# Paged sample attention: one block of scores per sequence, laid over four groups of 32 rows, in place of four blocks of 32 rows

## Chip, cores and metric

The kernel is one inference step of a decoder layer on one core of a Trainium2 chip. The metric is device time in microseconds (us), the median of several executions. Engines are named as in the profile: PE (TensorE matmul), PEld (its weight load), DVE (VectorE), ACT (ScalarE), POOL (GpSimd), SP (the engine that issues most DMAs).

## What is computed

The layer has a front projection, attention for a prompt of 1024 rows, attention for 8 sample sequences against paged caches, an output projection and an expert layer. The change is in the sample attention alone. In the reference it is, for each of the 8 sequences (16 pages of 128 cached rows, 4 new positions, 8 heads):

```python
def one_seq(args):
    pages, qb, cb, rb = args
    c_past = cache_kv_latent[pages].reshape(-1, KV_LORA)
    r_past = cache_k_rope[pages].reshape(-1, QK_ROPE_DIM)
    ...
    k = mla_keys(c_all, r_all, w_uk, g_k_nope, g_k_rope)
    mask = jnp.arange(past + s)[None, :] <= (past + jnp.arange(s))[:, None]
    p = attn_probs(qb[None], k, mask)
    o_lat = jnp.einsum('bhql,blc->bqhc', p.astype(c_all.dtype), c_all)
    return jnp.einsum('bqhc,chv->bqhv', o_lat, w_uv)[0]
```

`mla_keys` normalises each key over 96 numbers, of which 64 come from the latent row through `w_uk` and 32 from the rotary cache. `attn_probs` is a softmax over 2052 columns. All data is float32.

## The kernel before

`sample_attention` handles the 8 sequences b one after the other, each in 16 page steps p. The 4 positions by 8 heads make SQ = 32 query rows. PE makes, for each page, the page's keys of all heads (`d_kn`, line 786: two matmuls with 512 columns, into one of two PSUM banks) only to get their norms: ACT squares them (`d_sq`, line 883, two buffers) and DVE sums them per head (line 948). The scores themselves are made without the keys, from queries that were multiplied with `w_uk` ahead (`d_qa`): every fourth page, `group(c)` makes the scores of four pages in three matmuls of 512 columns into 32 rows of one of two banks (lines 777 and 778), and ACT copies them to `s_row` (line 889), 32 rows of 2052 columns.

The softmax of a sequence is its tail, and runs a piece at a time within the page steps of the next sequence: each engine's `tail` returns a table from page number to piece. On PE: the inverse norms are turned page by page into rows (line 812, 16 matmuls at pages 1 and 2), the probabilities are turned page by page (line 827, 16 matmuls at page 6), the latent rows are multiplied with them (lines 837 and 838, 17 matmuls of 256 columns at page 7), the result is turned (line 844, page 9). On DVE: four products of scores and norms (line 972), the row maximum (986), 1/sum and the scaling of the result (993, 997). ACT takes the exponential (line 904).

Within DVE's page steps stand the steps of the expert gather, 20 per sequence: each waits for a 512 KB row block that POOL fetched with an indirect DMA (line 126) into one of five buffers, and takes one pass over it (lines 141 and 148); POOL fetches into a buffer once DVE has used it.

SP issues the page loads. `load_keys` (line 728) issues 32 DMAs for a sequence, `load_latents` (lines 732 and 734) 17. The keys of sequence n+1 are issued once the scores of sequence n-1 are made, since both use one of two buffers; its latents once the latent product of n-1 is made (`d_lat`). PE begins the stage when `d_w_ukT` has landed (semaphore `d_ukt`), and waits at page 4 of the first sequence for the other 12 pages of keys. Order on each engine is the order written here; nothing reorders it.

Of the kernel before, what the change touches and what calls it, by code (L numbers as in the profile page):

```python
# [16 lines left out]
P = 128  # L17
# [633 lines left out]
def sample_attention(nc, a, qk_s, kept, gather, steps, gelus):  # L651
# [3 lines left out]
    SQ = DEC_S * H  # L655
    with ExitStack() as ctx:
        def sb(name, shape, dt=F32):
# [4 lines left out]
        w_ukT = sb("d_w_ukT", [NOPE, H, KVL])  # L662
        eps = sb("d_eps", [P, 1])
# [12 lines left out]
        s_new = [sb(f"d_snew{e}", [DEC_S, SQ]) for e in range(2)]  # L676
        rows = [sb(f"d_rows{e}", [P, PAST + DEC_S]) for e in range(2)]
        s_row = [r[0:SQ, :] for r in rows]
        mx = sb("d_mx", [SQ, 1])
        nmx = sb("d_nmx", [SQ, 1])  # L680
        tot = sb("d_tot", [SQ, 1])
        inv = sb("d_inv", [SQ, 1])
        pT = sb("d_pT", [P, PAGES + 1, SQ])
        ol = sb("d_ol", [SQ, KVL])
        olT = sb("d_olT", [P, CT, H, NS])
        o = rows[0][0:NS, 0:H * VD]
        oT = rows[0][:, 512:512 + G4 * P].rearrange("p (k t) -> p k t", k=G4)
# [6 lines left out]
        s = with_sems(nc, ctx, """d_first0 d_first1 d_rest0 d_rest1 d_lt0 d_lt1 d_eps d_qg d_qap d_qa d_mm d_sq d_red d_sc d_raw d_krsq d_krss  # L694
            d_ks1 d_ks2 d_ks3 d_kinv d_new d_smask d_tr d_nb d_ntr d_nrow d_mx d_nmx d_exp d_inv d_ptr d_pt d_lat d_ol
            d_olt d_olT d_op d_o d_ot d_zero d_oT d_st d_ukt""")
# [3 lines left out]
        GROUPS = PAGES // 4  # L700
# [18 lines left out]
        def _(sp):  # L719
# [29 lines left out]
            sp.dma_start(a["mixT_d"][:, :, SEQ:NPAD], oT).then_inc(s["d_st"], 16)  # L749
# [7 lines left out]
        def _(pe):  # L757
            pe.wait_ge(s["d_qg"], 2)
            pe.wait_ge(s["d_ukt"], 16)
# [7 lines left out]
            def pages(b, e, n, tail):  # L767
                cols = slice(b * DEC_S, (b + 1) * DEC_S)
                some = slice(b * SQ, (b + 1) * SQ)

                def group(c):

                    after(pe, s["d_raw"], GROUPS * b + c - 1)
                    o = sc[c % 2][0:SQ, :].rearrange("q (p l) -> q p l", l=P)
                    four = slice(4 * c, 4 * c + 4)
                    for k in range(CT):
                        pe.matmul(o, qa[:, k, some], page[e][:, four, k * P:(k + 1) * P], start=k == 0, stop=False)
                    pe.matmul(o, qr[:, some], krT[e][:, four, :], start=False, stop=True).then_inc(s["d_sc"], 1)
                for p in range(PAGES):
# [9 lines left out]
                    if p % 4 == 3:  # L789
                        group(p // 4)  # L790
# [1323 lines left out]
```

## Time and profile before

| | |
|---|---|
| median of 3 executions | 3730.46 us (3698.07 to 3737.71) |
| profiled execution: span from first to last instruction | 3729.2 us |
| PE busy | 3092.1 us (83%) |
| DVE busy | 2760.2 us (74%) |
| POOL, ACT busy | 1769.9 us, 992.3 us |
| DMA over the span | 241 GB/s, 899.72 MB |
| sample attention | from about 952 to 1481 us of the span |

The profile gives of the profiled execution only its span; what lies around it is not shown, and the span stands 1.3 us below the median of the three. Times in the rows below are from the start of the span. In a row of instructions the first number is the start, the second the time covered, then engine, line, operation, output and inputs, shapes, and how many records were merged. A float32 matmul leaves two MATMUL records and two weight loads. An idle time ahead of a row stands in brackets with what ended it. A share of busy time is an average, so the stage's own rows are what counts here.

### The profile page before, as it was taken

Reading aid. Unit: us, or ns where it says so; the run is one execution under the profiler, and the core shown is the slowest. Engines: PE = TensorE matmul, PEld = TensorE weight load, DVE = VectorE, ACT = ScalarE, POOL = GpSimd, SP = SyncE. Lnnn points to the kernel's source line nnn. Section 1 sums busy time; section 2 is a strip of 40 time slices with the busy share of each in tenths; the row PEclk is TensorE's granted clock in tenths of the full one; section 3 lists DMA queues with packets and bytes.
Section 4 is the critical chain, followed back from the end, with each engine's and each line's share of the span. In section 5 each row is a group of like instructions: output and inputs, shape, how many; then the busy total and the mean of one; then the engine's idle time right before and its main releaser. Section 6 shows DMA issues by size and latency. Waiting matters only on the chain. (4 is left out here: it accounts for less than half of the span.)

```text
span 3729.2 us, 41634 instructions
## 1 busy us (share of the span) xinstructions
PE 3092.1 (83%) x13229; PEld 2245.2 (60%) x13229; DVE 2760.2 (74%) x5323; ACT 992.3 (27%) x1643; POOL 1769.9 (47%) x1379
## 2 busy tenths in 40 slices
PE   6655687887699997765774779999999999999997
PEld 3445344565344443434764667777777877787775
DVE  3237687578567673673999877888888888898887
ACT  2222122233223232111111663222222222222221
POOL 0025554256333341563564554556666655555553
PEclk9577798578799998777887899999999999999998
DMA  3221576378787773886100359999999999999987
GB/s 111 88 102 45 202 274 218 116 228 291 251 282 254 241 251 117 307 314 218 34 23 6 137 242 333 343 328 333 339 341 330 343 330 336 336 341 340 331 330 262
DMA packets 311725, 899.72 MB, mean 241 GB/s; under 512 B 34377, under 2 KB 125690, under 8 KB 301242
## 3 DMA queue, kind: packets, MB, share of 16 engines
q0 software_dynamic: 156672, 570.49, 43.3%
q1 hardware_dynamic: 152874, 323.74, 24.2%
q10 hardware_dynamic: 2016, 3.67, 0.3%
q8 instruction: 59, 0.97, 0.1%
q14 instruction: 104, 0.85, 0.1%
HBM read 844.38 MB, written 53.64 MB: 241 GB/s over the span
## 5 line engine op out<-in xcount | busy, mean ns | idle before, releaser
L126 POOL DMA_INDIRECT x_got<-v,x_expert x544 | 676.8, 1244 | 750.1 <-DVE x_y L148 609.4
L126 POOL DMA_INDIRECT x_got<-u_rows,x_expert x544 | 731.8, 1345 | 626.2 <-DVE x_got L141 477.7
L148 DVE SCALAR_TENSOR_TENSOR x_y<-x_got,x_hidden,x_y 128x1024 f32<-128x1024 f32 x544 | 695.4, 1301 | 40.7 <-DMA x_got<-v,x_expert 31.7
L141 DVE SCALAR_TENSOR_TENSOR x_got<-x_got,x_y 128x1024 f32<-128x1024 f32 x544 | 646.8, 1220 | 37.9 <-DMA x_got<-u_rows,x_expert 36.5
L1735 PE MATMUL e_a<-h2h,e_uh 128*128 128x512 f32 x1024 | 406.5, 397 | 53.9 <-DVE e_ul L1815 34.3
L1737 PE MATMUL e_a<-h2h,e_ul 128*128 128x512 f32 x1024 | 401.1, 392 | 0.0
L1736 PE MATMUL e_a<-h2l,e_uh 128*128 128x512 f32 x1024 | 400.7, 391 | 0.0
L1780 ACT ACTIVATE e_vh<-e_v 128x2048 fp32r<-128x2048 f32 x64 | 122.5, 1915 | 567.6 <-PE e_yt L1754 544.7
L1735 PEld LDWEIGHTS e_a<-h2h,e_uh 128*128 128x128 f32 x1024 | 193.4, 189 | 115.3 <-issue 57.6
L786 PE MATMUL d_kn<-w_uk_kept,d_page 128*128 128x512 f32 x512 | 254.6, 641 | 9.5 <-DMA d_krT<-page_krT 8.7
L1737 PEld LDWEIGHTS e_a<-h2h,e_ul 128*128 128x128 f32 x1024 | 193.3, 189 | 41.1
L1736 PEld LDWEIGHTS e_a<-h2l,e_uh 128*128 128x128 f32 x1024 | 193.5, 189 | 38.7
L1752 PE MATMUL e_y<-e_wh,e_vh 128*128 128x512 f32 x512 | 201.6, 394 | 5.8 <-DVE e_wl L1835 5.7
L1754 PE MATMUL e_y<-e_wh,e_vl 128*128 128x512 f32 x512 | 200.5, 392 | 0.0
L1753 PE MATMUL e_y<-e_wl,e_vh 128*128 128x512 f32 x512 | 200.4, 391 | 0.0
L1753 PE MATMUL e_yt<-e_wl,e_vh 128*128 128x512 f32 x512 | 199.6, 390 | 0.0
L1752 PE MATMUL e_yt<-e_wh,e_vh 128*128 128x512 f32 x512 | 199.6, 390 | 0.0
L948 DVE TENSOR_REDUCE d_kss<-d_sq 128x8 f32<-128x512 f32 x128 | 87.0, 679 | 152.0 <-ACT d_sq L883 152.0
L1754 PE MATMUL e_yt<-e_wh,e_vl 128*128 128x512 f32 x512 | 199.3, 389 | 0.0
L1821 DVE TENSOR_TENSOR e_vl<-e_v,e_vh 128x2048 fp32r<-128x2048 f32 x64 | 146.4, 2288 | 44.4 <-ACT e_vh L1780 44.4
L1815 DVE TENSOR_TENSOR e_ul<-e_u,e_uh 128x1024 fp32r<-128x1024 f32 x128 | 156.6, 1223 | 28.5 <-ACT e_uh L1775 28.2
L786 PEld LDWEIGHTS d_kn<-w_uk_kept,d_page 128*128 128x128 f32 x512 | 96.7, 200 | 131.8 <-issue 119.8
(394 smaller groups left out, 5937.8 us busy)
## 6 DMA issues: line engine op xcount, KB each, us to landing
e_u<-uT SPq DMA_DIRECT2D x128, 512.0 KB, 6.9
e_v<-v SPq DMA_DIRECT2D x64, 1024.0 KB
gates_d<-g_stage SPq DMA_DIRECT2D x8, 4096.0 KB, 11.8
e_gate<-gates_d SPq DMA_DIRECT2D x32, 1024.0 KB
d_page<-page SPq DMA_DIRECT2D x128, 144.0 KB, 3.5
d_latent<-page_rows SPq DMA_DIRECT2D x128, 128.0 KB
x_got<-u_rows,x_expert POOLq DMA_INDIRECT x544, 5.9
x_got<-v,x_expert POOLq DMA_INDIRECT x544, 6.0
```

The source lines that it names most:

```text
L126: pool.indirect_dma_start(out=self.got[row][:], out_offset=None, in_=self.tables[phase], in_offset=bass.IndirectOffsetOnAxis(ap=self.exper ...
L141: dve.scalar_tensor_tensor(out=row[:], in0=row[:], scalar=1.0, in1=self.y[g][:], op0=ALU.mult, op1=ALU.mult, accum_out=self.hidden[:, g, k ...
L148: dve.scalar_tensor_tensor(out=self.y[g][:], in0=row[:], scalar=self.hidden[:, g, k:k + 1], in1=self.y[g][:], op0=ALU.mult, op1=ALU.add).t ...
L786: mm = pe.matmul(kn[p % 2][:, :], page[e][:, p, k * P:(k + 1) * P], w_uk[:, k, :], start=k == 0, stop=k == CT - 1)
L1735: pe.matmul(o, uh[q][:, k, :], h2h[:, k, :], start=k == 0, stop=False)
L1736: pe.matmul(o, uh[q][:, k, :], h2l[:, k, :], start=False, stop=False)
L1737: mm = pe.matmul(o, ul[q][:, k, :], h2h[:, k, :], start=False, stop=k == KD - 1)
L1752: pe.matmul(o, h, wh[r][:, :], start=begins and c == 0, stop=False)
L1753: pe.matmul(o, h, wl[r][:, :], start=False, stop=False)
L1754: mm = pe.matmul(o, l, wh[r][:, :], start=False, stop=ends and c == 3)
L1815: dve.tensor_tensor(ul[r][:], u[j % U_RING][:], uh[r][:].bitcast(F32), ALU.subtract).then_inc(s["e_ul"], 1)
L1821: dve.tensor_tensor(vl[:, two, :], v[:], vh[:, two, :].bitcast(F32), ALU.subtract).then_inc(s["e_vl"], 1)
```

## The change

The 128 partitions are cut into PARTS = 4 groups of 32 rows, and page 4c+j belongs to group j, block c. The scores of a sequence are no longer made in four blocks: after its last page PE makes them all in 12 matmuls of 512 columns, which write group j of one bank, so that `s_row` has 128 rows of 516 columns. The inverse norms and the probabilities are then turned by four whole 128x128 transposes each. The latent product has the same 17 matmuls, but block c of group j adds into rows 32j to 32j+31 of `lat`. Since a query's scores now stand in four rows, its maximum and its sum have to be joined over groups. For the maximum PE turns the 128 row maxima into one row (`maxima`), DVE takes the maximum over the groups (`top`), PE spreads it (`spread`, four matmuls) and ACT scales it (`nmx`). For the sum there is one matmul with a constant matrix `same`, which is loaded by a new DMA that PE waits for at the start of the stage. The matmuls that turn the result join the groups through `same` too. ACT copies the scores once per sequence, and the tail's pieces stand at other pages.

```diff
+    PARTS = P // SQ
+    GROUPS = PAGES // PARTS
...
+        same = sb("d_same", [P, P])
...
-        s_row = [r[0:SQ, :] for r in rows]
+        s_row = sb("d_rows", [P, GROUPS * P + DEC_S])
+        prob = sb("d_prob", [P, GROUPS * P + DEC_S])
+        top = sb("d_top", [1, SQ])
+        pT = sb("d_pT", [P, GROUPS, P])
...
-        sc = [bank("d_sc0"), bank("d_sc1")]
-        misc = [bank("d_m0"), bank("d_m1")]
+        sc = bank("d_sc")
+        norm = bank("d_nb")
+        turn = bank("d_pt")
         new = bank("d_new")
         lat = bank("d_lat")
+        small = bank("d_small")
+        new_sc = new[0:DEC_S, 0:SQ]
+        new_turn = new[:, P:P + DEC_S]
+        new_prob = new[0:DEC_S, 2 * P:2 * P + SQ]
+        mx_row, mx_col, tot_col = small[0:1, 0:P], small[:, P:P + 1], small[:, 2 * P:2 * P + 1]
...
             load_keys(0, 0)
+            sp.dma_start(same[:], a["same"]).then_inc(s["d_ukt"], 16)
             load_keys(1, 1)
             load_latents(0, 0)
             load_latents(1, 1)
             for n in range(1, DEC_B - 1):
                 e = (n - 1) % 2
                 sp.wait_ge(s["d_krsq"], n)
-                sp.wait_ge(s["d_raw"], GROUPS * n)
+                sp.wait_ge(s["d_sc"], n)
...
+                after(pe, s["d_raw"], b)
+                for k in range(CT):
+                    for j in range(PARTS):
+                        pe.matmul(sc[j * SQ:(j + 1) * SQ, :].rearrange("q (c l) -> q c l", l=P), qa[:, k, some],
+                                  page[e][:, j:PAGES:PARTS, k * P:(k + 1) * P], start=k == 0, stop=False)
+                for j in range(PARTS):
+                    mm = pe.matmul(sc[j * SQ:(j + 1) * SQ, :].rearrange("q (c l) -> q c l", l=P), qr[:, some],
+                                   krT[e][:, j:PAGES:PARTS, :], start=False, stop=True)
+                mm.then_inc(s["d_sc"], 1)
             def tail(t, e, n):
...
+                def new_rows():
+                    pe.wait_ge(s["d_smask"], t + 1)
+                    pe.wait_ge(s["d_neg"], 2)
+                    after(pe, s["d_nrow"], t)
+                    pe.matmul(new_turn, s_new[e][:], ident[0:DEC_S, 0:DEC_S], start=True,
+                              stop=True).then_inc(s["d_ntr"], 1)
+                def norms():
                     pe.wait_ge(s["d_kinv"], t + 1)
...
+                    after(pe, s["d_nb"], t)
+                    for c in range(GROUPS):
+                        mm = pe.transpose(norm[:, c * P:(c + 1) * P],
+                                          kinv[:, c * PARTS:(c + 1) * PARTS, :].rearrange("p j q -> p (j q)"), ident[:])
                     mm.then_inc(s["d_tr"], 1)
...
+                def maxima():
+                    pe.wait_ge(s["d_mx"], t + 1)
+                    after(pe, s["d_inv"], t)
+                    pe.matmul(mx_row, mx[:], ident[:], start=True, stop=True).then_inc(s["d_mxr"], 1)
+                def spread():
+                    pe.wait_ge(s["d_top"], t + 1)
+                    after(pe, s["d_nmx"], t)
+                    for j in range(PARTS):
+                        mm = pe.matmul(mx_col[j * SQ:(j + 1) * SQ, :], top[:], ident[0:1, 0:1], start=True, stop=True)
+                    mm.then_inc(s["d_mxc"], 1)
                 def probs():
                     pe.wait_ge(s["d_exp"], t + 1)
...
+                    after(pe, s["d_pt"], t)
+                    for c in range(GROUPS):
+                        mm = pe.transpose(turn[:, c * P:(c + 1) * P], prob[:, c * P:(c + 1) * P], ident[:])
                     mm.then_inc(s["d_ptr"], 1)
...
+                    after(pe, s["d_ptn"], t)
+                    pe.matmul(new_prob, prob[0:SQ, GROUPS * P:GROUPS * P + DEC_S], ident[0:SQ, 0:SQ], start=True,
+                              stop=True).then_inc(s["d_ptr"], 1)
+                    after(pe, s["d_inv"], t)
+                    pe.matmul(tot_col, same[:], tot[:], start=True, stop=True).then_inc(s["d_totc"], 1)
                 def latent():
                     pe.wait_ge(latent_in[e], 16 * (PAGES + 1) * n)
...
+                    pe.wait_ge(s["d_pt"], t + 1)
+                    pe.wait_ge(s["d_ptn"], t + 1)
+                    after(pe, s["d_olT"], t)
+                    pe.matmul(lat[0:SQ, 0:KVL], pT_new[:], c_now[e][:], start=True, stop=False)
+                    for c in range(GROUPS):
+                        for j in range(PARTS):
+                            mm = pe.matmul(lat[j * SQ:(j + 1) * SQ, 0:KVL], pT[:, c, j * SQ:(j + 1) * SQ],
+                                           latent_rows[e][:, c * PARTS + j, :], start=c == 0 and j > 0,
+                                           stop=c == GROUPS - 1)
+                    mm.then_inc(s["d_lat"], 1)
                 def latent_turn():
                     pe.wait_ge(s["d_ol"], t + 1)
                     for k in range(CT):
...
+                        mm = pe.matmul(lat[:, KVL + k * SQ:KVL + (k + 1) * SQ], ol[:, k * P:(k + 1) * P],
+                                       same[:, 0:SQ], start=True, stop=True)
                     mm.then_inc(s["d_olt"], 1)
-                return {1: norms_first, 2: norms_rest, 6: probs, 7: latent, 9: latent_turn}
+                return {2: new_rows, 3: norms, 5: maxima, 6: spread, 9: probs, 11: latent, 13: latent_turn}
...
+                def raw():
+                    act.wait_ge(s["d_sc"], t + 1)
+                    after(act, s["d_exp"], t)
+                    act.activation(s_row[:, 0:GROUPS * P], sc[:, :], ACT.Copy).then_inc(s["d_raw"], 1)
...
+                    act.wait_ge(s["d_mxc"], t + 1)
+                    act.activation(nmx[:], mx_col, ACT.Copy, scale=-SM).then_inc(s["d_nmx"], 1)
+                    act.wait_ge(s["d_nmx"], t + 1)
                     act.wait_ge(s["d_nrow"], t + 1)
...
+                    after(act, s["d_ptr"], 2 * t)
+                    after(act, s["d_totc"], t)
+                    act.activation(prob[:], s_row[:], ACT.Exp, bias=nmx[:], scale=SM,
...
-                return {3: row_new, 5: exp, 7: probs, 10: latent_turn}
+                return {1: raw, 3: row_new, 7: exp, 10: probs, 14: latent_turn}
...
+                    dve.tensor_tensor(s_row[:, 0:GROUPS * P], s_row[:, 0:GROUPS * P], norm[:, :],
                                       ALU.mult).then_inc(s["d_nb"], 1)
...
+                    dve.wait_ge(s["d_nb"], t + 1)
+                    dve.wait_ge(s["d_nrow"], t + 1)
+                    after(dve, s["d_mxr"], t)
+                    dve.tensor_reduce(mx[:], s_row[:], AX, ALU.max).then_inc(s["d_mx"], 1)
                 def maximum():
...
+                    dve.wait_ge(s["d_mxr"], t + 1)
+                    after(dve, s["d_mxc"], t)
+                    dve.tensor_reduce(top[:], mx_row.rearrange("o (j q) -> o q j", j=PARTS), AX,
+                                      ALU.max).then_inc(s["d_top"], 1)
                 def latent():
...
+                    dve.wait_ge(s["d_totc"], t + 1)
+                    dve.reciprocal(inv[:], tot_col).then_inc(s["d_inv"], 1)
                     dve.wait_ge(s["d_inv"], t + 1)
                     dve.wait_ge(s["d_lat"], t + 1)
                     after(dve, s["d_olt"], t)
...
-                return {2: scaled_first, 3: scaled_rest, 4: maximum, 9: latent}
+                    dve.tensor_scalar(ol[:], lat[:, 0:KVL], inv[:], None, ALU.mult).then_inc(s["d_ol"], 1)
+                return {4: scaled, 6: maximum, 12: latent}
...
+        "same": np.tile(np.eye(DEC_S * H, dtype=f), (P // (DEC_S * H), P // (DEC_S * H))),
```

How the order moves, at the three places that matter. First PE, pages 1 to 7 of the second sequence, before (`d_m` holds turned norms and probabilities, `d_sc` scores, `d_lat` the latent product):

```order
L786 MATMUL d_kn<-w_uk_kept,d_page 128x512 x2
L812 MATMUL d_m<-ident_kept,d_kinv 32x128 x8
L786 MATMUL d_kn<-w_uk_kept,d_page 128x512 x2
L812 MATMUL d_m<-ident_kept,d_kinv 32x128 x8
L821 MATMUL d_new<-ident_kept,d_snew 32x4
L786 MATMUL d_kn<-w_uk_kept,d_page 128x512 x2
L777 MATMUL d_sc<-d_page,d_qa 32x512 x2
L778 MATMUL d_sc<-d_krT,d_qr 32x512
L786 MATMUL d_kn<-w_uk_kept,d_page 128x512 x6
L827 MATMUL d_m<-ident_kept,d_rows 128x32 x16
L830 MATMUL d_m<-ident_kept,d_rows 4x32
L786 MATMUL d_kn<-w_uk_kept,d_page 128x512 x2
```

The tail is done by page 9 there, and two of the four blocks of scores stand between its pieces.

The same sequence on PE after the change, from page 3 to page 11 (`d_nb` turned norms, `d_pt` turned probabilities, `d_small` maxima and sums):

```order
L825 MATMUL d_nb<-ident_kept,d_kinv 128x128 x4
L788 MATMUL d_kn<-w_uk_kept,d_page 128x512 x4
L832 MATMUL d_small<-ident_kept,d_mx 1x128
L788 MATMUL d_kn<-w_uk_kept,d_page 128x512 x2
L838 MATMUL d_small<-ident_kept,d_top 32x1 x4
L788 MATMUL d_kn<-w_uk_kept,d_page 128x512 x6
L845 MATMUL d_pt<-ident_kept,d_prob 128x128 x4
L848 MATMUL d_new<-ident_kept,d_prob 4x32
L851 MATMUL d_small<-d_tot,d_same 128x1
L788 MATMUL d_kn<-w_uk_kept,d_page 128x512 x4
L858 MATMUL d_lat<-d_c_now,d_pTn 32x256
L861 MATMUL d_lat<-d_latent,d_pT 32x256 x16
```

Sixteen matmuls for the norms and sixteen for the probabilities became four transposes each, the latent product moved from page 7 to page 11, and the pieces at pages 5 and 6 are new. Behind it, from page 12 to the end of the sequence:

```order
L788 MATMUL d_kn<-w_uk_kept,d_page 128x512 x4
L869 MATMUL d_lat<-d_same,d_ol 128x32 x2
L788 MATMUL d_kn<-w_uk_kept,d_page 128x512 x4
L805 MATMUL d_sc<-d_page,d_qa 32x512 x8
L808 MATMUL d_sc<-d_krT,d_qr 32x512 x4
```

The 12 score matmuls stand in one lump behind the last page.

DVE, the tail of the first sequence inside the second, after the change, with the gather steps (`x_got`) between:

```order
L976 TENSOR_REDUCE d_kss<-d_sq 128x8
L1000 TENSOR_TENSOR d_rows<-d_rows,d_nb 128x512
L1005 TENSOR_REDUCE d_mx<-d_rows 128x1
L141 SCALAR_TENSOR_TENSOR x_got,x_hidden<-x_got,x_y 128x1024
L976 TENSOR_REDUCE d_kss<-d_sq 128x8
L141 SCALAR_TENSOR_TENSOR x_got,x_hidden<-x_got,x_y 128x1024
L976 TENSOR_REDUCE d_kss<-d_sq 128x8
L1010 TENSOR_REDUCE d_top<-d_small 1x32
```

The four products at pages 2 and 3 became one at page 4 with the maximum right behind it, and the joined maximum `d_top` stands two pages later.

SP, after the change, at the end of the first sequence's keys:

```order
L738 DMA d_page<-page 128x288
L738 ISA
L738 DMA d_krT<-page_krT 32x128
L748 DMA d_same<-same 128x128
L732 TENSOR_LOAD table_kept
```

The load of `same` stands behind all 32 key loads of the first sequence; the one of `d_w_ukT` stands ahead of them as before.

## Rows read from the trace of the kernel before

**Rows 1.** Busy time in stretches of the stage; the first line names the columns
```profile
core 0: us, PE busy (x) PEld busy (x) DVE busy (x) ACT busy (x) POOL busy (x), PEclk, DMA share, GB/s
1018.50:1079.70 61.20, 60.28 (x214) 26.04 (x212) 41.97 (x72) 19.46 (x32) 24.11 (x21) 0.97 0.85 286
...
1140.70:1201.70 61.00, 60.08 (x209) 26.63 (x208) 41.86 (x50) 18.26 (x31) 23.32 (x21) 0.94 0.76 250
...
1445.70:1480.00 34.30, 24.44 (x136) 17.78 (x136) 7.25 (x11) 4.68 (x8) 0.00 (x0) 0.75 0.07 26
```

**Rows 2.** Waits, 960 to 1460 us: who waited for whom, total, times, longest
```profile
ACT d_sq L883 <- PE d_kn L786: 227.4, 107, 11.9
POOL x_got L126 <- DVE x_y L148: 218.5, 91, 12.7
DVE d_kss L948 <- ACT d_sq L883: 152.0, 41, 14.8
```

**Rows 3.** Timeline of PE, pieces of the second sequence
```profile
1018.95 1.99 PE L786 MATMUL d_kn<-w_uk_kept,d_page 128*128 128x512 f32 x4
1020.86 0.54 PE L795 MATMUL d_new<-qk_s 96*4 96x4 f32 x16
...
1023.25 1.93 PE L812 MATMUL d_m<-ident_kept,d_kinv 128*32 128x128 f32 x16
...
1030.92 1.90 PE L777 MATMUL d_sc<-d_page,d_qa 128*32 128x512 f32 x4
...
1033.72 5.42 PE L786 MATMUL d_kn<-w_uk_kept,d_page 128*128 128x512 f32 x12
1039.81 3.75 PE L827 MATMUL d_m<-ident_kept,d_rows 32*128 32x32 f32 x32 [0.67 <-ACT d_rows L904]
...
1043.52 3.66 PE L786 MATMUL d_kn<-w_uk_kept,d_page 128*128 128x512 f32 x4
...
1049.91 7.09 PE L837 MATMUL d_lat<-d_latent,d_pT 128*32 128x256 f32 x32
```

**Rows 4.** Transposes of 128x128 in the prompt attention, timeline of PE
```profile
887.01 1.04 PE L577 MATMUL t2a_t<-t2a_ident,t2a_p 128*128 128x128 f32 x8
```

**Rows 5.** Groups by line, 960 to 1460 us: busy us, mean ns, idle before
```profile
L148 DVE SCALAR_TENSOR_TENSOR x_y<-x_got,x_hidden,x_y 128x1024 f32<-128x1024 f32 x122 | 155.6, 1275 | 2.6
L948 DVE TENSOR_REDUCE d_kss<-d_sq 128x8 f32<-128x512 f32 x128 | 87.0, 679 | 152.0 <-ACT d_sq L883 152.0
L972 DVE TENSOR_TENSOR d_rows<-d_rows,d_m 32x512 f32<-32x512 f32 x32 | 20.4, 668 | 3.4 <-PE d_m L812 3.4
L986 DVE TENSOR_REDUCE d_mx<-d_rows 32x1 f32<-32x2052 f32 x8 | 18.2, 2269 | 0.0
```

**Rows 6.** Timeline of SP: first and last key load of a sequence, its latents
```profile
1091.27 0.33 SPq L728 DMA_DIRECT2D d_page<-page  x1
...
1116.73 0.33 SPq L728 DMA_DIRECT2D d_krT<-page_krT  x1
...
1120.43 17.09 SPq L734 DMA_DIRECT2D d_latent<-page_rows  x16
```

**Rows 7.** DMA queues, 960 to 1460 us: packets, MB, share of 16 engines
```profile
q0 software_dynamic: 22896, 83.37, 49.8%
q1 hardware_dynamic: 42546, 37.35, 23.9%
```

**Rows 8.** Timeline at the start of the stage, PE and SP
```profile
957.52 7.00 PE L762 MATMUL d_kn<-d_qg,d_w_ukT 64*128 64x32 f32 x32 [10.81 <-DMA d_w_ukT<-w_ukT]
...
980.53 0.33 SPq L728 DMA_DIRECT2D d_krT<-page_krT  x1
...
986.28 4.63 PE L786 MATMUL d_kn<-w_uk_kept,d_page 128*128 128x512 f32 x5 [8.73 <-DMA d_krT<-page_krT]
```

**Rows 9.** Timeline at its end: last score matmul on PE, last turned result on ACT
```profile
1441.93 1.04 PE L778 MATMUL d_sc<-d_krT,d_qr 32*32 32x512 f32 x2
...
1477.46 0.22 ACT L917 ACTIVATE d_olT<-d_m 128x64 f32<-128x64 f32 x1 [10.77 <-PE d_m L844]
```

More of the change, by code:

```diff
@@ L769, in pages @@
                 some = slice(b * SQ, (b + 1) * SQ)
[L771 to L778, printed above, removed]
                 for p in range(PAGES):
@@ L794, in pages @@
                         for h in range(H):
[L795 removed]
+                            mm = pe.matmul(new_sc[:, h * DEC_S:(h + 1) * DEC_S], qk_s[0:HD, H + h, cols],
                                            qk_s[0:HD, h, cols], start=True, stop=True)
@@ L799, in pages @@
                         tail[p]()
-            def tail(t, e, n):
-                def norms_first():
-                    pe.wait_ge(s["d_kinv"], t + 1)
-                    after(pe, s["d_olT"], t)
-                    after(pe, s["d_pt"], 2 * t)
-                    norms(0)
-                    norms(1)
-                def norms(c):
-                    for p in range(4 * c, 4 * c + 4):
-                        mm = pe.matmul(misc[c % 2][0:SQ, (p % 4) * P:(p % 4 + 1) * P], kinv[:, p, :], ident[:],
-                                       start=True, stop=True)
-                    mm.then_inc(s["d_tr"], 1)
-                def norms_rest():
-                    for c in (2, 3):
-                        pe.wait_ge(s["d_nb"], GROUPS * t + c - 1)
-                        norms(c)
-                    pe.wait_ge(s["d_smask"], t + 1)
-                    pe.transpose(new[0:SQ, 2 * SQ:2 * SQ + DEC_S], s_new[e][:],
-                                 ident[0:DEC_S, 0:DEC_S]).then_inc(s["d_ntr"], 1)
+                after(pe, s["d_raw"], b)
@@ L824, in probs @@
                 def probs():
                     pe.wait_ge(s["d_exp"], t + 1)
-                    for p in range(PAGES):
-                        mm = pe.matmul(misc[0][:, p * SQ:(p + 1) * SQ], s_row[e][:, p * P:(p + 1) * P],
-                                       ident[0:SQ, 0:SQ], start=True, stop=True)
+                    after(pe, s["d_pt"], t)
+                    for c in range(GROUPS):
+                        mm = pe.transpose(turn[:, c * P:(c + 1) * P], prob[:, c * P:(c + 1) * P], ident[:])
@@ L833, in latent @@
                 def latent():
                     pe.wait_ge(latent_in[e], 16 * (PAGES + 1) * n)
-                    pe.wait_ge(s["d_pt"], 2 * t + 2)
-                    for p in range(PAGES):
-                        pe.matmul(lat[0:SQ, 0:KVL], pT[:, p, :], latent_rows[e][:, p, :], start=p == 0, stop=False)
-                    pe.matmul(lat[0:SQ, 0:KVL], pT[0:DEC_S, PAGES, :], c_now[e][:], start=False,
-                              stop=True).then_inc(s["d_lat"], 1)
+                    pe.wait_ge(s["d_pt"], t + 1)
@@ L935, in _ @@
                               ALU.mult).then_inc(s["d_qg"], 1)
+            for e in range(2):
+                dve.memset(s_new[e][:], NEG).then_inc(s["d_neg"], 1)
+            dve.memset(oT[:], 0.0).then_inc(s["d_zero"], 1)
             def pages(b, e, n, tail):
```

94 lines of the change are left out of this document (28 added, 66 removed).

## The prediction

> **What bounds the kernel now.** I read the busy times by stretch first. In a sequence of the sample attention PE is busy 60 of 61 us, DVE 42, POOL 23, and the DMA engines 0.76 to 0.85 of the time [rows 1]. The waits say the same: ACT waited 227 us for PE's page keys, DVE 152 us for ACT's squares, and POOL 218 us for DVE to give back a buffer [rows 2], while DVE's pass over a fetched block had 2.6 us of idle time ahead of it in all [rows 5]. So PE paces this stage, the gather follows, and work taken from PE is worth time there until DVE, SP's issuing or the DMA engines take over. The stages behind it only start earlier. Seven sequences run from 1018.95 us [rows 3] to the end of the last scores at 1442.97 us [rows 9], which is 60.6 us for each.
>
> **PE per sequence.** A page is four records, 12 of them take 5.42 us [rows 3], so 1.77 us for a page with its handover and 28.3 us for 16. The scores cost per block 1.9 for four records and 0.93 for two more [rows 3, 9], 11.2 us in all. Norms cost 2 x 1.9, probabilities 0.67 + 3.75, the page behind them 3.66 in place of 1.77, since the granted clock was at the lower level there, the latent product 7.6 with the new row, and the rest about 1.3 [rows 3]. The sum is 58.
>
> After the change the page keys stay at 28.3. Norms and probabilities become four transposes each, and four took 1.04 us [rows 4]. The small pieces (maxima, spread, the sum through `same`, the new row) are under 20 records; 16 tiny records took 0.54 us [rows 3], so 0.7 us, and with `d_new` and the turned result 1.8 us. The scores still are 24 records of 512 columns and the latent product 34 of 256. What four column groups do is not in this trace: no two matmuls here write different groups of 32 rows. Above, they run one after the other: 24 x 0.46 = 11 us and 7.6 us, as now [rows 3]. Below, four at a time: 2.8 and 2 us. I take a value between. A float32 matmul is two records over the same columns, so the second of one matmul cannot share its columns' group with the first, but can run beside the first record of the next group's matmul. 24 records then fill 13 slots, 6 us, and 34 fill 18, 4 us. PE's sum is 28.3 + 2.1 + 1.8 + 6 + 4 = 42 us (51 with no overlap, 37 with full overlap).
>
> The Trainium skill (TensorE: Matmul & The Clock Gate, part 3, on packing small matmuls) says that matmuls in different column groups run at once but start and end in program order, and gives 2.38x for three column tiles. By that factor, as an estimate, the scores would take 4.7 us; no run here shows it, and the sequence's time below would be the same.
>
> **DVE per sequence.** It was busy 41.9 us [rows 1]. Four products of 0.668 us over 32 rows become one of the same width over 128 rows, and the maximum of 2052 columns, 2.27 us, becomes one of 516, about the 0.68 us of a 512-column reduction [rows 5]. With a small one for `top` (0.2) that is 4.9 - 1.6 = 3.3 us less: 38.6. Two places add about 1.5 us: the maximum must wait for the product just ahead of it, and the Sqrt on ACT at the sequence's end is waited for as now. That makes 40.
>
> **The new waits.** At page 5 PE waits for DVE's maximum, which stands behind DVE's page 3, and at page 6 for `top`, behind DVE's pages 4 and 5. Behind it on PE are pages 6 and 7, which DVE will want. DVE then holds two pages of squares not yet summed and up to three gather steps, 1.28 + 0.68 us a page [rows 5], so some 4 us of work, while PE needs 1.8 us for a page and ACT another 0.6: covered as long as fetched blocks are there. Without that cover it would cost some 2 us a sequence. The ACT chain behind it (scale, Exp) has three pages until PE's probabilities at page 9. The scores' lump holds back the next page 0 by 6 us; DVE has its last two pages, the end of the sequence and a gather step, about 8 us, to do in the meantime. With 11 us of lump it would stand idle some 5 us.
>
> **SP.** A sequence's 32 key loads take 1091.27 to 1117.06, 25.8 us, and its 17 latent loads 18.4 us [rows 6], together 44 us per sequence at the least. The latents now start behind page 11 and not 7: at about 33 us of a 48 us sequence, ending at 52, so the next keys start 4 us late. They are wanted 48 us after that sequence's start and need 26, so this hides.
>
> **DMA.** Over 500 us the two queues took 49.8% and 23.9% of the 16 engines [rows 7], that is 368 us, or 46 us per sequence. None of this traffic goes away. So 46 us is the floor if the engines never pause, above DVE's 40, SP's 44 and PE's 42. The highest share in these stretches is 0.85 [rows 1], which would make 54 us, but PE was holding the gather back there. I take 48 (0.96 busy), nearer to the floor, since five buffers of fetches and SP's loads compete at all times. With the two bounds the range for a sequence is 46 to 54.
>
> **Start and end.** PE now waits for `same` too. It is issued behind the keys whose last load goes out at 980.53 us, and those keys had landed at 986.28 [rows 8], so PE starts at about 987 and not 957.5. It then does its 7 us of queries, ACT copies them, and page 0 runs at the lower clock (a page took 3.66 at it [rows 3]): DVE gets its first squares at about 999.5. All keys are there by then, so 16 pages at DVE's pace of 36 us (no tail inside yet) and the lump end at about 1037. Before, it was 1018.95: a loss of 18 us, bounded by 15 and 23 (no overlap). At the end, the last tail has no pages to hide in. It took 1442.97 to 1477.68, 34.7 us [rows 9]. The change takes from it 2.8 us for norms, 2 for products, 1.6 for the maximum, 2.7 for probabilities, 3.6 for latents [rows 3 to 5] and 1.4 for an exponential a quarter as wide, and adds about 2 us of handovers for the joined maximum: 12 us less (8 with no overlap).
>
> **Sum.** +18 - 7 x (60.6 - 48) - 12 = -82 us. The span of 3729.2 becomes 3647; the median shown lies 1.3 us above the span, so 3648.
>
> **Rivals.**
> 1. The column groups do not overlap, and the change buys only what the transposes and the wider tail give. For it: nothing in the trace shows two groups at once. PE has 51 us of work and some 2 us of waits for DVE: 53 us a sequence. +22 - 7 x 7.6 - 8 = -39: 3691.
> 2. PE's clock. The page behind the probabilities ran at 1.2 GHz, 3.66 us in place of 1.77 [rows 3], and in the stage's end, with PE busy 24.4 of 34.3 us, the granted clock was 0.75 against 0.94 to 0.97 [rows 1]. PE now waits at pages 5 and 6 and idles more, so more pages may run at the lower level. Each costs 1.9 us. With no overlap and 53 us a sequence, the kernel gets slower from 58.6 us on, at three such pages; six make 64.4 us, +22 + 7 x 3.8 - 8 = +41: 3771. With overlap it takes over nine pages to lose anything. Against it: where PE has work it stays near 0.95, and with no overlap it has work nearly all the time.
> 3. The DMA engines stay at 0.85, as fetches through five buffers leave gaps: 54 us, +18 - 46 - 12 = -40: 3690. Against it: in no stretch was the gather itself waited for [rows 2, 5].
>
> **How the numbers follow.** The forecast, with overlap at least in pairs and 46 to 51 us a sequence (3632 to 3669), has 0.60; rival 1 has 0.25 (3680 to 3705), rival 2 has 0.08, rival 3 has 0.07. Start and end unknowns widen the forecast to 3620 on the low side. The range of 3620 to 3704 leaves out rival 2 and the edges of the others. About 1% is what can be told from no change, so faster means below 3693: all of the forecast, half of rival 1 and most of rival 3, 0.76; within 1%, 0.16; slower, rival 2, 0.08.
>
> **What would show it.** Right: sequences start 48 us apart, DVE's waits for ACT's squares nearly vanish, the DMA share is 0.9 or more in every sequence, the 24 score records take about 6 us and the 34 latent records 4, and PE's first matmul of the stage starts near 987. Wrong: the 24 records take 10 us or more (rival 1), pages of 3.6 us in number (rival 2), DVE waiting for fetched blocks at a DMA share of 0.85 (rival 3).

## The result, and the profile after

The changed kernel takes 3601.8 us (median of 4 executions, 3584.1 to 3612.8) where the kernel before took 3717.9 (median of 4; three of them gave the 3730.5 from which the forecast was worked out). The ratio is 0.967, with a 95% interval of 0.963 to 0.971: faster, as forecast, and by more than the range allowed (low end 3620). Medians and ratios below are of executions in the faster of two states; one of experiment 6, 9649 us, is left out by that.

In the profiled executions below the sample attention starts anywhere from 917.8 to 956.9 us of the span with the same work ahead of it, so whole times of single executions scatter. What is compared below is therefore the **stage**: from SP's issue of `d_w_ukT` to ACT's last `d_olT`. Before, it ran from 952.74 to 1477.46 us [rows 9], 524.7 us; after, from 956.9 to 1355.38, 398.5 us. The span fell by 118.2 us (3729.2 to 3611.0), 8 less than the stage: the stage begins 4.2 us later, and some 4 are lost behind it. A **gap** is the time from one sequence's rotary score matmuls to the next's; it was 60.6 us before.

Of the stage's -126.2 us, the first sequence brought +7.2 (its lump ends 73.4 us behind the stage's start, before 66.2), the seven gaps -115.5 (41.2, 41.6, 41.6, 47.0, 45.2, 47.0, 44.8: mean 44.1) and the last tail -17.9 (16.8 us for 34.7). The prediction had +18, -88 and -12.

The busy times by stretch of the kernel after, columns as in [rows 1]; the first stretch is the second sequence, the last one lies in the sixth and seventh:

```profile
1030.26:1071.51 41.25, 37.26 (x170) 15.84 (x166) 39.09 (x70) 15.59 (x29) 25.68 (x21) 1.00 1.05 385
1071.51:1113.10 41.59, 37.27 (x171) 15.85 (x167) 39.74 (x48) 15.04 (x28) 24.70 (x21) 1.00 1.02 360
1200.00:1250.00 50.00, 44.22 (x204) 18.40 (x197) 41.63 (x52) 17.27 (x32) 27.41 (x22) 0.93 0.96 340
```

Against [rows 1], PE is down from 60 to 37 us a sequence and DVE from 42 to 39. The number to look at is the next to last: the DMA share passes 1.0 at 385 GB/s, where before 0.85 stood beside 286 GB/s. Later the granted clock falls a little (0.93) and the rate too, as PE pauses there.

PE in that second sequence, columns as in [rows 3]:

```profile
1040.16 0.60 PE L825 MATMUL d_nb<-ident_kept,d_kinv 128*128 128x128 f32 x4
...
1045.13 0.38 PE L832 MATMUL d_small<-ident_kept,d_mx 128*1 128x128 f32 x2 [0.94 <-DVE d_mx L1005]
...
1048.80 0.24 PE L838 MATMUL d_small<-ident_kept,d_top 1*32 1x1 f32 x8 [1.37 <-DVE d_top L1010]
...
1054.22 0.60 PE L845 MATMUL d_pt<-ident_kept,d_prob 128*128 128x128 f32 x4
...
1055.14 3.68 PE L788 MATMUL d_kn<-w_uk_kept,d_page 128*128 128x512 f32 x8
1058.75 0.61 PE L858 MATMUL d_lat<-d_c_now,d_pTn 4*32 4x256 f32 x2
1059.29 1.93 PE L861 MATMUL d_lat<-d_latent,d_pT 128*32 128x256 f32 x32
1061.16 3.70 PE L788 MATMUL d_kn<-w_uk_kept,d_page 128*128 128x512 f32 x8
...
1068.67 1.92 PE L805 MATMUL d_sc<-d_page,d_qa 128*32 128x512 f32 x16
1070.52 1.06 PE L808 MATMUL d_sc<-d_krT,d_qr 32*32 32x512 f32 x8
1071.51 1.98 PE L788 MATMUL d_kn<-w_uk_kept,d_page 128*128 128x512 f32 x4
```

The 24 score records take 2.84 us from the start of the first to the start of the next page: the time of six, so four groups at once. The 32 latent records take 1.87 us to the next row's start (2.41 with the new row), where they took 7.09 before [rows 3]. The page behind the probabilities no longer runs at half the clock: there 8 records take 3.68 us, where 4 took 3.66 [rows 3]. The two waits for the joined maximum (0.94 and 1.37 us) are there, as foretold, and DVE did not wait for PE's pages behind them.

From the fourth sequence on, PE waits at page 4 in every one:

```profile
1124.42 5.40 PE L788 MATMUL d_kn<-w_uk_kept,d_page 128*128 128x512 f32 x8 [2.57 <-DMA d_krT<-page_krT]
```

The waits of the kernel after, 956 to 1356 us (who waited for whom, total, times, longest) [rows 2]:

```profile
ACT d_sq L908 <- PE d_kn L788: 191.7, 106, 10.5
POOL x_got L126 <- DVE x_y L148: 105.9, 74, 6.4
DVE d_kss L976 <- ACT d_sq L908: 63.2, 17, 38.9
PE d_kn L773 <- DMA d_same<-same: 36.4, 1, 36.4
PE d_kn L788 <- DMA d_krT<-page_krT: 26.7, 5, 6.8
```

DVE's wait for squares fell from 152 to 63 us, 38.9 of it one wait at the start. New is the last line: five waits for keys, one in each of sequences 4 to 8. Who makes the keys late stands in SP's timeline, first and last key load of a sequence, its latents and the next first key load [rows 6]:

```profile
1094.46 0.33 SPq L738 DMA_DIRECT2D d_page<-page  x1
...
1119.68 0.33 SPq L738 DMA_DIRECT2D d_krT<-page_krT  x1
...
1121.41 17.08 SPq L744 DMA_DIRECT2D d_latent<-page_rows  x16
1139.32 0.33 SPq L738 DMA_DIRECT2D d_page<-page  x1
```

SP waited for nothing inside the stage. A sequence's 49 issues take it from 1094.46 to 1139.32, 44.9 us, and the later loads up to 46.0; the last four gaps have a mean of 46.0. The last keys go out at 1119.68 and PE has them at 1124.42, where its wait ends, 4.7 us later; in the next four sequences it is 5.6 or 5.7 us. Nor is it traffic that slows the issuing: the first 32 key loads of the stage went out in 25.6 us (958.72 to 984.32) at 132 GB/s, these 32 in 25.6 (1094.46 to 1120.05) at 377.

The DMA queues, 960 to 1340 us, columns as in [rows 7]:

```profile
q0 software_dynamic: 22741, 82.82, 59.9%
q1 hardware_dynamic: 43232, 37.88, 31.7%
```

The same 121 MB moved, in 380 us and not 500, at a share that rose only from 74 to 92%. PE's timeline at the start of the stage and at its last scores [rows 8, 9]:

```profile
986.41 7.00 PE L773 MATMUL d_kn<-d_qg,d_w_ukT 64*128 64x32 f32 x32 [36.42 <-DMA d_same<-same]
...
1337.80 1.06 PE L808 MATMUL d_sc<-d_krT,d_qr 32*32 32x512 f32 x8
```

PE now starts 29.5 us behind the stage's begin, having waited for `same`. ACT's last turned result, which closes the stage [rows 9]:

```profile
1355.38 0.22 ACT L942 ACTIVATE d_olT<-d_lat 128x64 f32<-128x64 f32 x1 [5.96 <-PE d_lat L869]
```

From the start of the last scores to it are 17.6 us; before, there were 35.5 [rows 9].

### The profile page after: what moved, and what is told of

It is laid out like the page before. It is cut to its first block and busy times, and to the rows that moved or that the text cites. A ratio compares the mean times of both kernels' runs of the same rounds, so it can differ in the third digit from the quotient of the medians.

```text
span 3611.0 us, 40929 instructions
## 1 busy us (share of the span) xinstructions
PE 2940.8 (81%) x12893; PEld 2175.4 (60%) x12893; DVE 2731.0 (76%) x5301; ACT 966.1 (27%) x1627; POOL 1772.3 (49%) x1379
## 5 line engine op out<-in xcount | busy, mean ns | idle before, releaser
L126 POOL DMA_INDIRECT x_got<-v,x_expert x544 | 684.1, 1258 | 627.7 <-DVE x_y L148 480.8
L148 DVE SCALAR_TENSOR_TENSOR x_y<-x_got,x_hidden,x_y 128x1024 f32<-128x1024 f32 x544 | 695.6, 1302 | 45.2 <-DMA x_got<-v,x_expert 35.8
L788 PE MATMUL d_kn<-w_uk_kept,d_page 128*128 128x512 f32 x512 | 251.4, 635 | 29.7 <-DMA d_krT<-page_krT 26.7
L1866 DVE TENSOR_TENSOR y_turned<-e_yt,y_turned 128x512 f32<-128x512 f32 x124 | 85.6, 690 | 100.5 <-PE e_yt L1774 100.5
```

The lines of the kernel that those rows point to most:

```text
L126: pool.indirect_dma_start(out=self.got[row][:], out_offset=None, in_=self.tables[phase], in_offset=bass.IndirectOffsetOnAxis(ap=self.exper ...
L148: dve.scalar_tensor_tensor(out=self.y[g][:], in0=row[:], scalar=self.hidden[:, g, k:k + 1], in1=self.y[g][:], op0=ALU.mult, op1=ALU.add).t ...
L788: mm = pe.matmul(kn[p % 2][:, :], page[e][:, p, k * P:(k + 1) * P], w_uk[:, k, :], start=k == 0, stop=k == CT - 1)
```

## Experiments

The theory after the result was **A**: SP's issuing paces the sequences from the fourth on, and the first three escape it because their loads went out while PE waited 36 us for `same`. Its rivals were **B** (the start's 36 us add to the end) and **C** (the DMA engines' bandwidth is the bound, at a share near 1).

**1. `same` issued ahead of the first keys** (B against A)

```diff
-            load_keys(0, 0)
             sp.dma_start(same[:], a["same"]).then_inc(s["d_ukt"], 16)
+            load_keys(0, 0)
             load_keys(1, 1)
```

> The load of `same` is issued right behind `d_w_ukT`, ahead of the keys, so PE can start near 961 us in place of 986. Theory A (SP's issuing paces the stage: 44.7 us of issuing per sequence without a pause from 957 us on): the keys of sequences 3 to 8 arrive when they did, so the stage ends where it did and the time equals the changed kernel's within 4 us; PE waits longer for keys (26.7 us in 5 waits becomes about 40). Theory B (the start's delay is simply added to the end): 11 to 15 us less than the changed kernel. Theory C (the DMA engines are the bound): also no change, but without longer waits for keys.

Measured: 3597.8 us, 0.968 [0.962, 0.974]; the stage 398.5 us, as long as the change's. PE began 24.5 us earlier against the stage's start, and its waits for keys grew instead, from 26.7 us in 5 to 50.0 in 8 (gaps 42.6, 51.2, then 44.0 to 47.5). B falls: the start was no cost, the loads' own pace set the end.

**2. Less issuing on SP** (A against C): a third latent buffer, so that the latents of a page go out with its keys, and one reading of the page's number serves three DMAs. The bytes are the same.

```diff
-        latent_rows = [sb(f"d_latent{e}", [P, PAGES, KVL]) for e in range(2)]
+        latent_rows = [sb(f"d_latent{e}", [P, PAGES, KVL]) for e in range(3)]
...
-                load_keys(n + 1, e)
-                sp.wait_ge(s["d_lat"], n)
-                load_latents(n + 1, e)
+                after(sp, s["d_lat"], n - 1)
+                load(n + 1, True, True)
```

> A third buffer of latent rows, so that SP issues a sequence's latents together with its keys and reads each page number once for three DMAs: about 36 us of issuing per sequence in place of 44.7, same bytes. Theory A (SP paces): the waits for keys vanish and all sequences take the 41.3 us that the first two took, DVE being the next bound: 7 x 2.7, about 18 us less than the changed kernel (12 to 22). Theory C (DMA engines, whose busy share is 0.96 to 1.05 now, are the bound): no change, within 4 us.

Measured: 3572.6 us, 0.959 [0.953, 0.965]; the stage 379.5, 19.0 shorter, and the gaps 40.2 to 42.9 us. SP's timeline, from the first issue of one sequence's load to that of the next, then a stretch by busy time:

```profile
1069.71 0.31 SPq L736 DMA_DIRECT2D d_c_now<-kv_all  x1
...
1107.65 0.31 SPq L736 DMA_DIRECT2D d_c_now<-kv_all  x1
```

```profile
1106.50:1146.90 40.40, 37.74 (x174) 15.81 (x170) 37.59 (x47) 15.11 (x29) 21.79 (x20) 1.00 1.05 383
```

49 issues in 37.9 us and not 44.9, and the gaps fall until SP itself waits for PE's scores (12.9 us in 4 waits). The DMA engines, at a share of 0.96 to 0.97 in the change's later sequences, moved 383 GB/s in place of 327 to 340. So they were not the bound there, C falls for the change, and A holds. The third buffer itself took no wait away, as SP had none for `d_lat` in the change.

**3. Both together**

> Both edits. Theory A: with SP out of the way the start counts again: 18 us from the issuing and 10 to 14 from the start, about 30 us less than the changed kernel (22 to 36). Theory C: no change against the changed kernel within 4 us. Theory B alone: the same 11 to 15 us as the load of `same` alone.

The edit is that of 1 and of 2. Measured: 3569.5 us, 0.960 [0.953, 0.967]; the stage 378.6, shorter by 19.9 and not by 30. PE's timeline in it, at page 4 of the third sequence:

```profile
1044.57 6.35 PE L787 MATMUL d_kn<-w_uk_kept,d_page 128*128 128x512 f32 x8 [13.37 <-DMA d_krT<-page_krT]
```

That gap was 53.8 us, those behind it 40.4 to 40.8. What the earlier start gave is paid back in one wait for keys. This kernel still loads the first sequence's latents apart and behind the second's keys; in experiment 6, which does not, the wait there is 2.9 us.

**4. No overlap of groups**: the records of one group all ahead of the next group's, scores and latents.

```diff
-                for k in range(CT):
-                    for j in range(PARTS):
-                        pe.matmul(sc[j * SQ:(j + 1) * SQ, :].rearrange("q (c l) -> q c l", l=P), qa[:, k, some],
...
+                    for k in range(CT):
+                        pe.matmul(o, qa[:, k, some], page[e][:, j:PAGES:PARTS, k * P:(k + 1) * P], start=k == 0, stop=False)
+                    mm = pe.matmul(o, qr[:, some], krT[e][:, j:PAGES:PARTS, :], start=False, stop=True)
...
-                    for c in range(GROUPS):
-                        for j in range(PARTS):
+                    for j in range(PARTS):
+                        for c in range(GROUPS):
```

> The changed kernel with the loops of the scores and of the latent product turned round: all matmuls of one column group, then all of the next. Nothing else moves. Theory D (PE starts matmuls in program order, and four groups run side by side because neighbours in the order lie in different groups): the 24 score records take 9 to 10.5 us in place of 2.85 and the 34 latent records 6 to 7.5 in place of 2.4; PE then has about 49 us a sequence and paces it at 49 to 51: 35 to 50 us more than the changed kernel, still some 65 to 80 less than the kernel before. Theory E (PE runs ahead across groups whatever the order): no change.

Measured: 3650.3 us, 0.979 [0.973, 0.985]; the stage 446.5, 48.0 longer than the change's, the first gap 49.1 and every other 49.6. PE, the latent product and the first two groups' scores:

```profile
1054.74 4.59 PE L859 MATMUL d_lat<-d_latent,d_pT 128*32 128x256 f32 x32
...
1066.78 1.91 PE L806 MATMUL d_sc<-d_page,d_qa 128*32 128x512 f32 x4
1068.61 1.04 PE L807 MATMUL d_sc<-d_krT,d_qr 32*32 32x512 f32 x2
1069.58 1.90 PE L806 MATMUL d_sc<-d_page,d_qa 128*32 128x512 f32 x4
1071.42 1.04 PE L807 MATMUL d_sc<-d_krT,d_qr 32*32 32x512 f32 x2
```

Four times 2.80 us make 11.2, the price without overlap, and PE was busy 48.2 of 49.6 us. So at least 48 of the stage's 126 us come from the overlap of groups, and at most 78 from the rest of the change. The latent product still overlapped in part (4.59 us, between 1.87 and 7.09).

**5. The order within a shape**: as the changed kernel, but the sixteen 128-row score records group by group, the rotary ones last.

```diff
-                for k in range(CT):
-                    for j in range(PARTS):
+                for j in range(PARTS):
+                    for k in range(CT):
```

> The changed kernel with one pair of loops turned round: the eight 128-row score matmuls are ordered by group (two of group 0, then two of group 1, ...), the four rotary ones stay behind them. With all loops turned round the 24 score records took 11.2 us, but there 128-row and 32-row matmuls also alternated; the 32 latent records took 4.6 in place of 1.9, and 6.8 one after the other. If PE can start a later group's matmul only when few are pending, the 16 records take about 3 to 5 us here in place of 1.85. If the alternating shapes alone caused the 11.2, they take 1.9 to 2.2. If there is no overlap at all in this order, 6.9.

Measured: 3602.5 us in one execution, the stage 399.6. PE's timeline at the scores:

```profile
1061.33 1.94 PE L805 MATMUL d_sc<-d_page,d_qa 128*32 128x512 f32 x16
1063.20 1.06 PE L808 MATMUL d_sc<-d_krT,d_qr 32*32 32x512 f32 x8
1064.19 1.98 PE L788 MATMUL d_kn<-w_uk_kept,d_page 128*128 128x512 f32 x4
```

The sixteen take 1.87 us in this order too, so group order alone does not keep records apart. A change of shape does so in every trace here: the rotary records (32 weight rows) start where the 128-row records end, also where they write other groups, as at 1069.58 above. That fits experiment 4's scores. Six records to a group in place of four are no better reason: with eight to a group, and one shape, experiment 4's latent product still overlapped in part.

**6. One load for everything**: experiment 2's load for the first sequence too, with `same` ahead of it.

```diff
-            load_keys(0, 0)
             sp.dma_start(same[:], a["same"]).then_inc(s["d_ukt"], 16)
-            load_keys(1, 1)
-            load_latents(0, 0)
-            load_latents(1, 1)
+            load(0)
+            load(1)
```

> Keys and latents of every sequence, the first two too, are issued together with one reading of the page number, and `same` is issued first. Measured from the issue of `d_w_ukT` to the last `d_olT`, the stage took 524.7 us before, 398.5 changed, 379.5 with less issuing and 378.6 with `same` first as well, where PE waited 13.4 us for the keys of the third sequence. Theory A (issuing is what the early sequences wait for): that wait goes, the stage takes 370 to 375. Rival (the DMA engines are full in the first two sequences, whatever the order): 377 to 381.

Measured: 3577.5 us (median of 3), 0.957 [0.952, 0.962]; the stage 370.3, the shortest of the kernels that compute everything, and 28.2 below the change's. Its gaps are 42.8, then 40.5 to 41.0.

**7. What sets the 40.5 us?** In that kernel PE is busy 37.5 us a sequence, DVE 38.4, SP issues for 35 to 40, and the DMA engines move 374 to 386 GB/s. One suspect after the other was made lighter: DVE's pass (`self.width` is half a row in this stage; one of its two lines is shown), then PE's page keys as well. Both kernels leave out a part of the computation, and each ran once (3585.1 and 3552.5 us).

```diff
-                dve.scalar_tensor_tensor(out=row[:], in0=row[:], scalar=1.0, in1=self.y[g][:], op0=ALU.mult,
+                dve.scalar_tensor_tensor(out=row[:, 0:self.width], in0=row[:, 0:self.width], scalar=1.0, in1=self.y[g][:, 0:self.width], op0=ALU.mult,
```

> Leaves out half of the columns in DVE's pass over the blocks fetched during this stage; every transfer stays. DVE's work falls by some 20 x 0.6 = 12 us a sequence to about 27, so it is no longer the bound. If DVE sets the 40.6 us of a sequence, PE is next with 37.3 busy: 37.5 to 39. If the DMA engines set it (share 1.03 to 1.05, 375 GB/s), a sequence stays at 40 to 41.

```diff
-                    for k in range(CT):
-                        mm = pe.matmul(kn[p % 2][:, :], page[e][:, p, k * P:(k + 1) * P], w_uk[:, k, :],
-                                       start=k == 0, stop=k == CT - 1)
+                    mm = pe.matmul(kn[p % 2][:, :], page[e][:, p, 0:P], w_uk[:, 0, :], start=True, stop=True)
```

> As the one with the lighter DVE pass, and it also leaves out the second of the two matmuls of each page's keys: PE falls by some 13 us to 24, DVE is at 27, SP issues for some 36 us a sequence. What is left is the DMA engines and SP. By the prediction's reading of the busy share (46 us of 16 engines per sequence) a sequence could not go below 46; all runs so far say that is wrong. If 385 to 390 GB/s, the highest seen, is what the engines can do, 15.2 MB take 39 to 40 us. If they can do more, SP's issuing sets 36 to 37.

With the light DVE pass the gaps became 52.7, 37.0, 44.2, 37.0, 41.9, 37.0, 48.9 (stage 379.6), with both 45.4, 40.8, 38.9, 47.0, 37.4, 44.6, 36.4 (stage 373.0). With the light DVE pass a sequence without a wait for keys takes 37.0 us, PE's own work, so DVE had set the 40.5. The kernel of experiment 6 says the same in its last sequence, where the DMA engines had less to move and the gap stayed:

```profile
1264.20:1304.70 40.50, 37.31 (x174) 15.88 (x172) 39.46 (x48) 15.08 (x29) 24.61 (x22) 1.00 0.84 286
```

But with the light pass the keys come late every other time, and nothing is gained. Late keys looked like issuing again; the second kernel suggests otherwise. SP's last key issue of one sequence in it:

```profile
1198.83 0.33 SPq L742 DMA_DIRECT2D d_krT<-page_krT  x1
```

And PE's wait for those keys:

```profile
1212.16 3.78 PE L781 MATMUL d_kn<-w_uk_kept,d_page 128*128 128x512 f32 x4 [13.84 <-DMA d_krT<-page_krT]
```

The row starts where the wait ends, so PE gets them at 1212.16, 13.3 us behind the issue. In the changed kernel it was 4.7 to 5.7, and its page loads took 4.7 us from issue to landing in the median:

```profile
d_page<-page SPq DMA_DIRECT2D x127, 144.0 KB, 4.7
```

PE had begun to wait at 1198.32, 0.5 us ahead of the issue; for the rest of the wait the loads were on their way. This sign alone proves little, since the latents stand between the keys here, as in experiment 6, where the same time was 9.6 to 11.0 us in the third to sixth sequence.

**8. Fewer bytes, the same issues** (DMA bytes against SP's issuing): on the kernel with the light DVE pass, and on that of experiment 6. From the fourth sequence on only 16 of the 128 rows of each latent page are loaded, another part that is left out.

```diff
+                        rows = slice(0, P // 8) if b > 2 and sem is latent_in[b % 3] else slice(None)
-                        sp.dma_start(dst[:, p, :], src[bass.ds(phys, 1)].rearrange("o p c -> (o p) c")
+                        sp.dma_start(dst[rows, p, :], src[bass.ds(phys, 1)].rearrange("o p c -> (o p) c")[rows, :]
```

> The kernel with DVE's gather pass at half its columns, and of the latent pages of sequences 4 to 8 only 16 of 128 rows are loaded (both are parts of the computation that it leaves out), with the same 49 issues on SP for a sequence. In the run with the light DVE pass the last five gaps were 44.2, 37.0, 41.9, 37.0 and 48.9 us (mean 41.8) at 376 to 388 GB/s, so some 15.7 MB each. Theory F, the DMA engines' bytes set what remained: 1.84 MB less at the same rate take 4.8 us, so the gaps fall to 37 to 38.5, PE's own 37.0, its waits for keys are below 2 us from sequence 4 on, and the stage is 362 to 368 us in place of 379.6. Theory G, SP's issuing sets it: the number of issues is the same, so the gaps stay at 41 to 43 in the mean with waits for keys of 4 to 12 us, and the stage at 378 to 382.

> The version with one load for all data of a sequence, in which of the latent pages of sequences 4 to 8 only 16 of 128 rows are loaded (a part of the computation that it leaves out); DVE's work is whole. Its gaps were 40.5 to 41.0 us at 374 to 386 GB/s. Theory H, DVE's work sets these gaps (38.4 us busy): they stay at 40.2 to 41.0 with a lower DMA rate of some 335 GB/s, and the stage at 368 to 371 us. Theory F, the DMA engines set them: they fall to 38 to 39.5, and the stage to 358 to 365.

Measured, in one execution each (3560.6 and 3584.7 us). Light DVE pass and fewer bytes: gaps 37.0 to 37.1 from the second on, no wait for keys behind the second sequence, the stage 355.9 us, even below the 362 to 368 expected, since the long last gap (48.9) went too. Whole DVE work and fewer bytes: gaps 48.3, then 39.3 to 40.6, the stage 371.2 (the first gap, whose loads are those of experiment 6, was 5.5 us longer in this execution). A stretch of the first by busy time:

```profile
1098.30:1135.30 37.00, 37.00 (x170) 15.80 (x166) 28.69 (x47) 14.99 (x29) 19.90 (x20) 1.00 1.03 365
```

And one of the second:

```profile
1106.30:1145.60 39.30, 37.23 (x171) 15.87 (x167) 37.14 (x46) 15.18 (x29) 22.74 (x20) 1.00 0.98 339
```

So with a light DVE the bytes were the bound (with the rows their packets went too; the two were not told apart), and in experiment 6 DVE sets the gap: freeing the DMA engines (from 374 to 386 GB/s down to 333 to 339) took only some 0.7 us of the mean of the last six gaps (40.7 to 40.0). The two limits stand close together: a sequence of experiment 6 moves some 15.5 MB (40.7 us at 382 GB/s), which at 385 GB/s take some 40 us.

## Why the prediction was wrong, point by point

**The step that failed is "46 us is the floor if the engines never pause".** It took the queues' share of busy time [rows 7] for a part of a capacity: 74% of 500 us, hence 46 us for each of eight sequences. Two things are wrong with that. The busy time of the same bytes is not fixed: it was 368 us for the 121 MB before and 348 after (91.6% of 380), 43.5 a sequence; from 0.76 at 250 GB/s [rows 1] to 1.05 at 385 the share rose by 38% and the rate by 54%. And the share does not end at 1: the second sequence had 1.05 over 41.25 us, 43.3 us of busy time, and stood below the floor from the start. In experiment 8's first kernel it was 1.03 where PE waited for no keys. A floor by bytes, at the highest slice of the stage, 395 GB/s, would have been 38 us for 15.1 MB (121.06 MB over eight). The Trainium skill (DMA: Bandwidth & Descriptors, Specifications) gives 435 GB/s as the fabric's ceiling and 358 as HBM's limit for a core; the runs here go above the second and stay below the first.

**What took its place is SP's issuing, a term that the prediction had.** It put SP at 44 us a sequence "at the least", below the floor, and reckoned the latents' delay hidden in a sequence of 48 us. Measured were 44.9 us, and experiment 2 took 7 us of issuing away and 19 us off the stage. That the mean gap of 44.1 equals this term is in part luck: three gaps of 41.2 to 41.6, with the lead that the start gave, stand beside four with a mean of 46.0. With the false floor struck out, the prediction's own terms (42, 40, 44) would have given 44 in place of 48, and 7 x 4 = 28 us less: 3620. The stage came out 44 us below the forecast's -82: 27 of them lie in the gaps, 11 in the start and 6 in the tail.

**Overlap in pairs was too cautious.** Forecast were 6 us for the scores and 4 for the latents with their new row, measured 2.84 and 2.41; the lower bounds were 2.8 and 2. Four transposes took 0.60 us, not 1.04. PE came to 37 us a sequence, the prediction's sum for full overlap, and not to 42. That moved little in the change, where SP decides, but it is why experiments 2 and 6 could reach 40.5. By the Trainium skill's 2.38x for three column tiles (TensorE: Matmul & The Clock Gate, part 3) the scores would have taken 4.7 us, as an estimate; here four groups gave four times. Its rule that matmuls start and end in program order would keep experiment 5's scores from overlapping fully, since the four records of one group follow each other; the 1.87 us speak against it. The Trainium skill (TensorEngine Tiling (Array Packing), Tiling Modes) says that a switch of tiling mode drains the engine, which agrees with experiment 4's 11.2 us.

**The start's +18 was +7, and it was no loss.** PE's first matmul came at 986.41 (forecast 987) and DVE's first squares at 998.67 (999.5), but that is in part luck: the stage began 4.2 us later than before, and `same` was there 2.1 us behind its issue at 984.32, so against the stage's start PE began at 29.5 us where some 34 were forecast. But I let DVE pace the first sixteen pages (36 us and the lump), and PE did: it was busy 33.9 of the 36.1 us from its first page to the lump's end. Experiment 1 shows that the delay itself cost the change nothing: the loads used it as their lead.

**The tail's -12 was -17.9.** In it the latent product took 3.41 us where it had taken 8.79, the norms 0.66 for 5.31 and the probabilities 1.11 for 7.03. The trace of before has these pieces longer than within a sequence (7.09, 3.8 and 3.75 us [rows 3]), at a granted clock of 0.75 [rows 1], and I had priced them as within a sequence: 3.6 us off the latents, and 5.4 came.

**What held:** the direction, DVE at 40 us (39 to 40 busy in the early gaps), the waits at pages 5 and 6, both there and both covered. Rival 1 (no overlap, 53 us a sequence) did not come; experiment 4 built nearly that and got 49.6 us, with PE at 48.2. Rival 2 (pages at the lower clock) did not come either: the granted clock was 0.88 to 1.00 in the sequences. Rival 3 (a DMA share of 0.85) fails with the floor.

## What to carry to other kernels

A share of DMA busy time is no capacity: take bytes over the highest rate that the same mix reaches, and keep the issuing engine's own time as a bound beside it. When a load is late, measure from its issue to the wait's end, beside what a load of that kernel takes otherwise: here some 5 us went with late issuing and 13 us with full queues, and only fewer bytes at the same issues settled it. A gain from overlap shows only until the next bound, so write down all of them: in experiment 6 four (PE, DVE, SP, bytes) lay within some 4 us of one another.

## What was not expected of the hardware

Four column groups overlapped fully for two-record float32 matmuls (24 records in 2.84 us), the sixteen of one shape in either order; with a change from 128 to 32 weight rows in every group none of it was left (11.2 us). In experiment 4's latent product (4.59 us), read record by record, the groups start at 1054.74, 1055.64, 1056.53 and 1057.42, 0.89 us apart: the time of four of a group's eight records (0.22 us each). So a group began when four records of the one ahead of it were left, ahead of records that stand earlier in the order; what is said ahead of the prediction, that nothing reorders an engine's instructions, does not hold for PE here. What sets the four was not tried. A DMA share above 1.0 stood over whole sequences. In the kernel with both parts light SP's issuing slowed with the traffic: 49 issues took 36.3 us (921.74 to 958.07, from first key load to first key load) at the start, and up to 45.5 us (1155.58 to 1201.10) later, with 0.4 us of waits in all; single issues that mostly took 0.33 us took up to 1.95.
